# A hybrid retention and mixture-of-experts layer on one core: paired weight transfers, one f32 down chunk, and biases added by VectorE

## The reference, cut to what matters

```python
def expert_block(args):
    xblk, e = args
    gu = xblk @ w_gu[e] + b_gu[e]                       # (rows, 1024) @ (1024, 2048)
    x_glu = jnp.minimum(gu[:, :F], SWIGLU_LIMIT)
    x_lin = jnp.clip(gu[:, F:], -SWIGLU_LIMIT, SWIGLU_LIMIT)
    act = x_glu * jax.nn.sigmoid(SWIGLU_ALPHA * x_glu) * (x_lin + 1.0)
    return act @ w_down[e] + b_down[e]                  # (rows, 1024) @ (1024, 1024)
```

## Time and profile before

| quantity | value |
|---|---|
| median of 3 executions | 1267.26 us |
| the profiled execution: its own time | 1267.78 us |
| the profiled execution: span | 1266.0 us |
| TensorE (PE) busy | 1160.1 us, 92% |
| VectorE (DVE) busy | 1128.3 us, 89% |
| ScalarE (ACT) busy | 924.4 us, 73% |
| GpSimd (POOL) busy | 509.2 us, 40% |
| moved by DMA | 458.07 MB, mean 362 GB/s |
| granted TensorE clock, mean over the span | 0.99 |

### The profile page before, as it was taken

The page is one execution under the profiler, slowest core; times in us unless marked ns, Lnnn a source line. Parts: engine busy times, 40 slices in busy tenths (PEclk is TensorE's granted clock), DMA queues, the critical chain, the costliest instruction groups (busy, mean ns, idle before and its releaser), DMA issues.

```text
span 1266.0 us, 39786 instructions
## 1 busy us (share of the span) xinstructions
PE 1160.1 (92%) x17462; PEld 894.8 (71%) x17463; DVE 1128.3 (89%) x849; ACT 924.4 (73%) x819; POOL 509.2 (40%) x69
## 2 busy tenths in 40 slices
PE   5999999789999999999999999999999999999984
PEld 2455544777777777777777777777888777777741
DVE  5742454789999999999999999999999999999988
ACT  5332432579888888888888888888888888888852
POOL 0120300006666666666665551111166666622400
PEclk9999999799999999999999999999999999999998
DMA  9609331699999999999999999999999999999986
GB/s 350 218 20 353 126 134 58 229 371 378 420 416 416 418 413 417 418 418 417 416 417 414 419 418 418 414 418 413 415 416 419 417 411 420 418 412 409 418 324 255
DMA packets 73254, 458.07 MB, mean 362 GB/s; under 512 B 10076, under 2 KB 10588, under 8 KB 23632
## 3 DMA queue, kind: packets, MB, share of 16 engines
q1 hardware_dynamic: 68480, 445.30, 86.5%
q0 software_dynamic: 3472, 8.21, 1.7%
q10 hardware_dynamic: 1152, 2.19, 0.5%
HBM read 443.26 MB, written 24.77 MB: 370 GB/s over the span
## 4 chain that ended last, share of the span: by engine, by line
PE 44%; DVE 29%; issue 17%; DMA 6%; ACT 2%; DVEq 0%; SPq 0%; ACTq 0%; POOLq 0%
DVE ring L399 20%; PE ps L420 15%; PE ps L456 10%; PE ps L1093 8%; PE ps L1194 4%; PE ps L413 3%; DMA ring<-in_w_down_dram 2%; DMA arena<-in_w_down_dram 1%; DVE arena L492 1%; ACT ring L396 1%; DVE arena L486 1%; DVE arena L489 1%; DMA ring<-in_w_gu_dram 1%; DVE arena L501 1%; DVE arena L495 1%
## 5 line engine op out<-in xcount | busy, mean ns | idle before, releaser
L478 POOL DMA_INDIRECT planes<-arena,slot_row x31 | 484.2, 15619 | 586.8 <-ACT arena L508 586.8
L399 DVE SCALAR_TENSOR_TENSOR ring<-ring 128x2048 f16<-128x2048 f32 x290 | 657.5, 2315 | 15.0 <-ACT ring L396 14.7
L396 ACT ACTIVATE ring<-ring 128x2048 f16<-128x2048 f32 x290 | 543.1, 1905 | 46.4 <-DMA ring<-in_w_gu_dram 22.9
L420 PE MATMUL ps<-arena,ring 128*128 128x88 f16 x12288 | 505.1, 205 | 46.2 <-issue 27.8
L420 PEld LDWEIGHTS ps<-arena,ring 128*128 128x128 f16 x12288 | 489.2, 100 | 55.9 <-issue 43.2
L456 PE MATMUL ps<-ring,arena 128*88 128x512 f16 x1536 | 338.0, 379 | 5.6 <-DVE arena L501 2.6
L456 PEld LDWEIGHTS ps<-ring,arena 128*88 128x88 f16 x1536 | 181.4, 120 | 148.6 <-issue 6.0
L399 DVE SCALAR_TENSOR_TENSOR ring<-arena,ring 128x2048 f16<-128x2048 f32 x94 | 214.4, 2316 | 0.9 <-ACT ring L396 0.9
L396 ACT ACTIVATE ring<-arena 128x2048 f16<-128x2048 f32 x94 | 178.0, 1904 | 12.4 <-DMA arena<-in_w_down_dram 6.5
L413 PE MATMUL ps<-arena 128*128 128x88 f16 x2048 | 94.2, 207 | 10.9 <-issue 7.6
L413 PEld LDWEIGHTS ps<-arena 128*128 128x128 f16 x2048 | 86.6, 101 | 12.0 <-issue 11.9
(11 more groups left out here) (153 smaller groups left out, 592.7 us busy)
## 6 DMA issues: line engine op xcount, KB each, us to landing
ring<-in_w_gu_dram SPq DMA_DIRECT2D x194, 1024.0 KB, 11.9
ring<-in_w_down_dram SPq DMA_DIRECT2D x96, 1024.0 KB, 12.1
arena<-in_w_gu_dram SPq DMA_DIRECT2D x62, 1024.0 KB, 12.5
arena<-in_w_down_dram SPq DMA_DIRECT2D x32, 1024.0 KB, 11.7
ring<-in_w_in_dram SPq DMA_DIRECT2D x4, 2048.0 KB, 12.4
ring<-planes SPq DMA_DIRECT2D x6, 1024.0 KB, 10.1
ring<-in_w_out_dram SPq DMA_DIRECT2D x2, 2048.0 KB, 8.5
arena<-in_x_dram SPq DMA_DIRECT2D x4, 512.0 KB, 11.6
```

Source lines behind the costliest of these rows:

```text
L396: return act.activation(split_of(slot)[:, 0, :], raw(r), ACT.Copy, scale=SCALE_W)
L399: return dve.scalar_tensor_tensor(split_of(slot)[:, 1, :], raw(r), SCALE_W, split_of(slot)[:, 0, :], ALU.mult, ALU.subtract)
L420: mm = pe.matmul(o, w[:, i, cols], src[:, j, k, :], start=start and n == 0, stop=stop and n == 2, skip_group_check=True)
L478: return pool.indirect_dma_start(out=planes, out_offset=bass.IndirectOffsetOnAxis(ap=rows, axis=0), in_=y_row[0:SCAT, :], in_offset=None, ...
```

## The change

Three things change together.

1. **Transfers in pairs.** `load_gu` and `load_dn` move 2 MB, two slots at once, so that each partition gets one run of 16 KB. ScalarE waits on the pair's semaphore. SyncE waits until both slots of a pair are free. A partition now holds four neighbouring rows of `w_down` or two of `w_gu`; `gu_cols` steps by 4 f16 and `pe_gather` by 2 to match.
2. **One down chunk unsplit.** From expert 3 on (its down product is in stage 4), except for the last expert, chunk 8 gets no high and low part. TensorE multiplies it in f32 straight from its raw slot with `nat`, an f32 copy of a quarter of the activations that ScalarE makes after `act_ah`. Its raw slot is freed by TensorE (`chunk_used`); the next tenants of that slot's pair are chunks 4 and 5 of the following stage, and SyncE waits for it there.
3. **Biases by VectorE.** `pe_bias` and its operands go. The biases are loaded at the start by ScalarE's queue, transposed by four PE transposes after the second `turn_qk`, and copied to `bguT` by four VectorE copies. Per expert, one VectorE step over 1408 columns reads PSUM, scales and adds the bias into SBUF; it frees the PSUM sums. The two clamps then run SBUF to SBUF, after one more low part.

```diff
+        def unsplit(h, q, c):
+            return c == GU_CH and not (isinstance(h, int) and h < 2)
+        def raw_free(eng, h, q, c):
+            s = 2 * h + q
+            if c == GU_CH + SLOTS - CH and not (isinstance(s, int) and s < 5):
+                eng.wait_ge(chunk_used, nth(s, c) - SLOTS + 1)
+            elif c >= SLOTS:
+                eng.wait_ge(low_ready, splits(s, c - SLOTS))
+            else:
+                eng.wait_ge(low_ready, splits(s - 1, c + CH - SLOTS))
         def load_gu(sp, k, e, slot):
-            return sp.dma_start(raw(slot),
-                                w_gu[0, bass.ds(e, 1), k * P:(k + 1) * P, :].rearrange("a p c -> (a p) c"))
+            src = w_gu[0, bass.ds(e, 1), k * P:(k + 2) * P, :].rearrange("a (p i) c -> (a p) (i c)", i=2)
+            return sp.dma_start(raw_pair(slot), src)
         def load_dn(sp, j, e, slot):
-            src = w_down[0, bass.ds(e, 1), 2 * j * P:2 * (j + 1) * P, :].rearrange("a (p i) c -> (a p) (i c)", i=2)
-            return sp.dma_start(raw(slot), src)
+            src = w_down[0, bass.ds(e, 1), 2 * j * P:2 * (j + 2) * P, :].rearrange("a (p i) c -> (a p) (i c)", i=4)
+            return sp.dma_start(raw_pair(slot), src)
...
-                    mm = pe.matmul(o, parts[:, i, t, d * P:(d + 1) * P], onehot[:, t, :],
+                    mm = pe.matmul(o, parts[:, i, t, spaced(d // 2 * 2 * P + d % 2, 2)], onehot[:, t, :],
...
-            return every_other(F * (j // 2) + 2 * b * P + j % 2)
+            return spaced(F * (j // 2) + b // 2 * 4 * P + b % 2 * 2 + j % 2, 4)
...
+        def pe_down_native(pe, r, f):
+            for half in range(2):
+                col = (f % 2) * D + half * 512
+                mm = pe.matmul(ROWS[:, half, :], nat[:, f * CAP:(f + 1) * CAP], raw(r)[:, col:col + 512],
+                               start=f == 0, stop=False, skip_group_check=True)
+            return mm
...
+        def dve_bias(dve, e):
+            return dve.scalar_tensor_tensor(
+                gub.rearrange("p b h (j c) -> p b (h j) c", j=2), GU.rearrange("p b (j c) -> p b j c", j=PER), UNSCALE,
+                bguT[:, bass.ds(e, 1), :].rearrange("p a (b j) -> p (a b) j", b=GB).unsqueeze(3)
+                .to_broadcast([P, GB, PER, CAP]), ALU.mult, ALU.add)
         def dve_glu(dve):
-            return dve.tensor_scalar(gub[:, :, 0], GU[:, :, 0:2 * CAP], LIM, UNSCALE, ALU.min, ALU.mult)
+            return dve.tensor_scalar(gub[:, :, 0], gub[:, :, 0], LIMIT, None, ALU.min)
         def dve_lin(dve):
-            return dve.tensor_scalar(gub[:, :, 1], GU[:, :, 2 * CAP:4 * CAP], LIM, -LIM, ALU.min, ALU.max)
+            return dve.tensor_scalar(gub[:, :, 1], gub[:, :, 1], LIMIT, -LIMIT, ALU.min, ALU.max)
...
+        def act_nat(act):
+            return act.activation(nat[:, :], gub[:, 0, 1, :], ACT.Copy, scale=SCALE_W)
...
-                    sp.wait_ge(low_ready, nth(s, c) - SLOTS + 1)
+                    raw_free(sp, h, q, c + 1)
+                    if c == GU_CH + SLOTS - CH:
+                        sp.nop()
+                        raw_free(sp, h, q, c)
...
             def down(s, j, c):
-                pe.wait_ge(low_ready, nth(s, c) + 1)
+                if unsplit(s // 2, s % 2, c):
+                    r = raw_slot(s // 2, s % 2, c)
+                    pe.wait_ge(nat_ready, s - 3)
+                    pe.wait_ge(slot_loaded[r // 2 * 2], loaded(s // 2, s % 2, c // 2 * 2))
+                    for f in range(2):
+                        mm = pe_down_native(pe, r, f)
+                    mm.then_inc(chunk_used, 1)
+                    return
...
             def stage(s, q, last=False, more_meta=True):
+                pe.wait_ge(xT_ready, 2 * s + 2)
                 pe.wait_ge(gu_taken, s)
-                pe_bias(pe, s)
-                pe.wait_ge(xT_ready, 2 * s + 2)
...
                     low(h, q, 10)
-                    taken(s, nth(s, GU_CH))
+                    biased(s, nth(s, GU_CH))
                     low(h, q, 11)
+                    clamped(s)
```

More of the change, by code:

```diff
@@ L153, in build_program @@
         ranks = sm[:, 384:384 + RANKS]
-        own_f = sm[:, 384 + RANKS:384 + RANKS + E]
         tri = sb("tri", [P, P], BF16)
         ones = sb("ones", [P, P], BF16)
[L157 to L161, removed]
+        wp_sb = sb("wp_sb", [P, H, P])
         wr_sb = sb("wr_sb", [P, KD, E])
         br_sb = sb("br_sb", [P, E])
+        rw_sb = sb("rw_sb", [P, W])
+        bguT = sb("bguT", [P, E, NF])
         ps_w = sb("ps_w", [P, H])
+        nat = sb("nat", [P, 2 * CAP])
         eps_t = sb("eps_t", [P, 1])
@@ L202, in build_program @@
         turned = [("x", t, i) for t in range(NT) for i in range(2)]
[L203 removed]
+        turned += [("qk", n) for n in range(2)] + [("bgu", j) for j in range(4)] + [("qk", n) for n in range(2, 8)]
         turned += [("s", h, i) for h in range(H) for i in range(NT)]
@@ L319, in build_program @@
         scattered = sem("scattered")
-        more = {k: sem(f"more_{k}") for k in ("high", "low", "used", "onehot", "gathered", "xT",
+        more = {k: sem(f"more_{k}") for k in ("high", "low", "used", "onehot", "gathered", "xT", "biased",
                                               "glu", "lin", "prod", "sig", "act32", "ah", "act",
@@ L430, in pe_meta, with spaced @@
             return mm
-        def every_other(first):
-            return slice(first, first + 2 * P - 1, 2)
+        def spaced(first, by):
+            return slice(first, first + by * P - by + 1, by)
         def gu_cols(b, j):
-            return every_other(F * (j // 2) + 2 * b * P + j % 2)
[L438 to L443, removed]
+            return spaced(F * (j // 2) + b // 2 * 4 * P + b % 2 * 2 + j % 2, 4)
         def pe_gu(pe, slot, q, k, b):
@@ L617, in _ @@
                 sp.dma_start(x_kept[t * P:(t + 1) * P, :], x_sb[:, t, :]).then_inc(kept_stored, 16)
-            for c in range(DN_CH, CH):
+            for c in range(DN_CH, CH, 2):
                 chunk(0, 1, c)
-            with sp.Fori(1, E // 2) as h:
+            for h in (1, 2):
                 for q in range(2):
-                    for c in range(CH):
+                    for c in range(0, CH, 2):
                         chunk(h, q, c)
-            for j in range(DN_CH):
+            with sp.Fori(3, E // 2) as h:
+                for q in range(2):
+                    for c in range(0, CH, 2):
+                        chunk(h, q, c)
+            for j in range(0, DN_CH, 2):
                 slot = raw_slot(E // 2, 0, j)
-                sp.wait_ge(low_ready, nth(E, j) - SLOTS + 1)
+                raw_free(sp, E // 2, 0, j + 1)
                 load_dn(sp, j, E - 1, slot).then_inc(slot_loaded[slot], 16)
@@ L631, in last_split @@
             def last_split():
-                sp.wait_ge(low_ready, CH * E)
+                sp.wait_ge(low_ready, splits(E, DN_CH - 1))
             def one(e, b, n):
-                for c in range(CH):
+                for c in range(0, CH, 2):
                     if c >= RAW:
-                        sp.wait_ge(more["low"], CH * (n - 1) + c - RAW + 1)
+                        sp.wait_ge(more["low"], CH * (n - 1) + c - RAW + 2)
                     ins = load_gu(sp, c, e, c % RAW) if c < GU_CH else load_dn(sp, c - GU_CH, e, c % RAW)
@@ L946, in act_high_part @@
                 act_ah(act).then_inc(ah_ready, 1)
+                if not (isinstance(e, int) and (e < 3 or e == E - 1)):
+                    act_nat(act).then_inc(nat_ready, 1)
             def stage(h, q, first=False, last=False):
@@ L1066, in _, with turn_bgu @@
             pe.wait_ge(small_loaded, 16)
+            def turn_bgu():
+                pe.wait_ge(bgu_loaded, 16)
+                for j in range(4):
+                    take(pe, ("bgu", j))
+                    pe.transpose(bank(("bgu", j))[:, 0:P], bgu_raw[:, spaced(j, 4)], ident).then_inc(bgu_turned, 1)
             def turn_x(t):
@@ L1440, in _, with turned_bgu @@
             low_win(1, 0)
+            def turned_bgu():
+                for j in range(4):
+                    dve.wait_ge(bgu_turned, j + 1)
+                    dst = bguT[:, :, :].rearrange("p e (ql b qh r) -> p e qh ql b r", ql=2, b=2, qh=2)[
+                        :, :, :, :, j // 2, j % 2]
+                    ins = dve.tensor_copy(dst, bank(("bgu", j))[:, 0:P].rearrange(
+                        "p (e qh ql) -> p e qh ql", e=E, qh=2))
+                    free(ins, ("bgu", j))
             def rotate(n):
@@ L1685, in _ @@
             low(0, 1, 2)
-            taken(0, GU_CH, first=True)
+            biased(0, GU_CH, first=True)
             low(0, 1, 3)
+            clamped(0)
             low(0, 1, 4)
```

106 lines of the change are left out of this document (55 added, 51 removed).

## The result

The changed kernel takes 1279.16 us (1277.94 to 1280.65, 4 runs) where the kernel before, run beside it, took 1266.76: a ratio of 1.0094, with a 95% interval of 1.0082 to 1.0105. It is slower by 12 us, 0.2 us above the upper end of the range; the forecast was 1261.5, a little faster than before.

What follows compares the result with a forecast made beforehand. VectorE paced 26 experts, then DMA, with TensorE close; after the change, DMA. From 1267.78 us: +1.7 before the experts, +2.4 for three stages, -7.0 for 27 stages, -3.0 slack: 1261.9, median 1261.5; range 1249 to 1279 us.

Steps and rivals of the forecast that it cites:

- VectorE's new pace: VectorE's time per expert after the change: one low part less, bias step more, 29.47 us (30.19 at the other end).
- The queue's pace at 16 KB runs: DMA time per expert: 31.13 to 31.40 us less 0.60 for longer runs, taken as 30.65 us.
- TensorE: TensorE's time per expert: 29.0 - 0.65 + 0.84 + 1.3 of gaps = 30.5 us, just behind DMA.
- Before the experts: Start of the kernel: earlier bias load and four more transposes cost +1.7 us, bounds nothing to +3.
- The slot costs nothing: Raw slot held for the f32 product: its loop fits the 30.65 us pace, with 4.3 us of backlog to spare.
- L + 19.0: Loop through one expert: landing time L plus 19.0 us of engine steps through the f32 product; L may be 11.6 us.
- The held slot as a rival: With L above 11.6 us, each expert pays every further us in full: 1291 us, chance 8%.
- The slack of 3.0 us: In the experts, VectorE running ahead at 29.47 us before DMA decides: 3 of 4.3 us taken, -3.0 us.
- The step of 8 bytes: Rival: TensorE's weight reads at a step of 4 f16 cost 5 ns each, +50 us in all, chance 5%.
- The queue gains more: Rival: fixed cost near 1.0 us per expert, DMA's pace 30.1, TensorE decides at 30.2: 1251 us, chance 12%.
- my line through two windows: DMA cost per run, from windows with 2 KB and 8 KB runs: 12.4 ns per run plus 0.0372 ns per byte.

Runs made afterwards that it cites:

- unsplit_bias: The changed kernel with single transfers of 1 MB and 8 KB runs instead of pairs: 1273.7 us.
- unsplit_last: The changed kernel with chunk 11 unsplit in place of chunk 8 and multiplied first: 1268.0 us.
- last_light: The changed kernel with chunk 11 unsplit and multiplied first, and 8 of TensorE's down matmuls per expert left out: 1264.2 us.
- no_hold: The changed kernel with the f32 product reading resident weights, so SyncE need not wait for TensorE to free the slot; true weights left out: 1267.2 us.
- hold_longer: The changed kernel with SyncE asking for chunks 4 and 5 only when TensorE is through with chunk 9, not 8: 1302.3 us.
- U: The unsplit f32 chunk; by itself, in the kernel before with single transfers and the old biases: 1295.1 us.
- B: The biases by VectorE; by itself, in the kernel before with twelve low parts and single transfers: 1290.4 us.
- unsplit_only: The kernel before with the unsplit f32 chunk alone, single transfers and the old biases: 1295.1 us.

## Why the prediction was wrong, step by step

- **VectorE's new pace.** Forecast 29.47 us; in unsplit_bias the sixth and seventh intervals are 29.46 and 29.47. Right, and with it the clamps at 0.44 us, the value I took against the other end of 0.80.
- **The queue's pace at 16 KB runs.** Forecast 30.65, from 31.13 or more minus 0.60. The 31.13 was right (31.12 in unsplit_bias), the gain was about 0.3 (30.8 in unsplit_last and last_light). The fixed cost of a run, drawn from two shares of two digits, was about twice too large. Mis-sized by 0.15 us, 4 us in all.
- **TensorE.** Forecast 30.5 with 1.3 us of gaps. Full in no_hold at 30.8: the gaps are 1.5, and 2.0 with the old biases. They were 1.3 only since a wait for VectorE stood in for some. Mis-sized by 0.3, and this left no slack.
- **Before the experts.** Forecast +1.7, measured +3.85. The bias part was exact. The pairs' 2.2 us are the step that I left out: I had written that a pair lands 2.5 us later and then asked only what the eight slots do with that in the experts, not who waits for a chunk ahead of them.
- **"The slot costs nothing."** This step failed, and with it the forecast: the slot costs 12 us (no_hold). The working was L + 19.0 against a pace of 30.65, so that L might be 11.6. L was not the mistake: the held pair lands after 8.7 us on average, near the 7.3 that I took and well under 11.6. The 19.0 was. From that landing to the end of the next f32 product it is 22.4 us on average, and 8.7 + 22.4, with 0.2 for the issue, is the 31.3 of a round. TensorE's gaps of 1.3 us were not in the 19.0, and the next pair was taken to be there in time, while it lands 5.2 us after the held one. How the 3.4 us divide between these is not settled. And I asked only whether the loop as a whole fits into the pace, not who has slack for a chunk that comes late in it: TensorE, full at 30.8 (no_hold), waits 0.5 us per expert for late low parts, and that is the 31.3.
- **The held slot as a rival.** Right in that the hold makes it slower, at 8%, wrong in its condition and its price. It wanted L above 11.6, and L is 8.7. It had each us paid in full, and hold_longer pays a third. What I set against it, that a late request shortens its own backlog, is not what saves the rest: 2.6 us more of hold shorten the landing by 0.1.
- **The slack of 3.0 us.** unsplit_bias has two intervals at 29.47; the changed kernel has one, at 29.48, followed by 33.24. Most of the 3.0 us did not come. That the hold took them back is not shown: no_hold, without the hold, has 30.18 and 30.11 in those two places.
- **The step of 8 bytes.** The rival fell: 240 matmuls in 9.40 us are 39.2 ns each, where the earlier trace rows has 40.4 at the step of 4 bytes. The Trainium skill's rule on 16-byte lines (SBUF — State Buffer, Door 1: The DMA port swizzle) agrees.
- **The queue gains more.** It fell too. The Trainium skill's 425 GB/s for a 16 MB transfer (DMA: Bandwidth & Descriptors, Where 436 GB/s comes from) was not reached here: 420 is the most that any window of 700 us shows.

## What to carry to other kernels

When three resources lie within 3% of each other, a part that relieves one of them can't be costed alone: U and B cost 27 and 23 us by themselves and 6 together. Before a buffer is handed to a later reader, add up the loop that it closes with every wait and gap in it and with the load that lands last, and ask which engine in it has no slack for a late chunk. Read the landing of the held load by itself: the median of all loads (12.2 here) is not that of the one that the loop runs through (8.7). Here it also paid to give the held buffer to the part that arrives last and is read first. A larger transfer makes its first half late: look for each engine that waits for that half with other work behind it.

## What the hardware showed that I had not expected

TensorE's "issue" gaps come from code loading, as far as the trace can say. The DMA view of no_hold, 400 to 700 us, has the instruction queue (packets, MB, share of 16 engines):

```profile
q8 instruction: 38, 0.62, 0.8%
```

That is four packets of 16 KB per expert, which take about 1.0 us each among the weights, where a packet of weights takes 0.63. In the DMA records of five kernels (before, changed, unsplit_only, unsplit_last, no_hold) all 187 issue gaps of TensorE between 400 and 1100 us end 1.15 to 1.65 us after the end of such a packet. That stretch of 0.5 us behind each of some 90 packets covers about 6% of the time, so it is hardly chance. No run removed the code loads, so the cause is read, not tested. The Trainium skill says that fetching the next block of code is mostly hidden behind issue (Runtime: NRT & Kernel Launch, Instruction fetch mechanics). If the gaps are the code loads, some 1.5 us per expert are not hidden here, 5% of TensorE's time.

A run of 8 KB takes 316 ns on its queue and one of 16 KB 626, in the DMA records of 400 to 1100 us before and after: 2 x 316 - 626 = 6 ns saved for each long one, not the 12.4 of my line through two windows.
